# Stick-breaking attention of a decoder trunk on one core: prompt heads taken in pairs, and the sample heads' blocks taken one after the other while cache pages are read

## The chip, the core and the metric

The kernel runs on one core of one Trainium2 chip. The metric is the time of one execution on the device, in microseconds (us); lower is better. The kernel before was run three times: 3911.35, 3921.86 (the median) and 3925.43 us.

## What is computed

The reference runs a decoder trunk of four layers over two groups of requests that share weights: one prompt of 512 tokens, and eight samples of 8 tokens each (64 tokens in all). Width is 1024, with 16 heads of 64. Layers 0 and 3 mix tokens by a short convolution, layer 2 by a recurrence, and layer 1 by stick-breaking attention, which is what the change touches. Every layer ends in a convolution FFN of width 2816. The attention, cut to what matters:

```python
z = einsum('bqhd,bkhd->bhqk', q_blk, keys) * HEAD_DIM ** -0.5 + bias
mask = k_pos[None, :] < q_pos[:, None]
log_stay = where(mask, log_sigmoid(-z), 0.0)
between = cumsum(log_stay, axis=3, reverse=True) - log_stay
a = where(mask, exp(log_sigmoid(z) + between), 0.0)
o = einsum('bhqk,bkhd->bqhd', a, vals)
```

So the weight of a key depends on the sum of softplus(z) over all later keys. The prompt attends to itself; each sample attends to 256 cached keys, held in two pages of 128 keys that a page table names, and to its own 8.

## The kernel before

The program is written by hand for five engines (TensorE, VectorE, ScalarE, GpSimd and SyncE) that run their own instruction lists in order and meet at semaphores. On chip, keys lie on partitions and queries along the free dimension; everything in the attention is float32. A matmul instruction in float32 leaves two passes, that is two LDWEIGHTS and two MATMUL records, in the trace; a transpose leaves one.

**Prompt attention** (functions `attention` of each engine). A head has four pieces, one for each block of 128 keys, taken from the last block to the first. The piece of block kb has the queries from that block on, so the widths are 128, 256, 384 and 512 columns. There are 64 pieces, head after head. For a piece, TensorE computes the scores from 64 rows of K and Q (`scores`, L715); VectorE adds the head's bias (L1762) and takes the absolute value (L1764); ScalarE takes Exp and Ln (L1293, L1295); VectorE completes softplus into `SP` (L1773); GpSimd sets the masked half of the first 128 columns to zero (`mask_sp`, L2198). Then TensorE adds to the scores, in the same PSUM bank, the softplus sums within the block (`cumulate`, matrix `ntri`, L723) and those over all later blocks (matrix `nones`, L727). For the latter, GpSimd keeps a running sum over the blocks, `SUM`, with a copy and an add per piece (L2203, L2205). ScalarE takes Exp with the bias (`weights`, L1303), GpSimd masks the first 128 columns again (`mask_a`, L2215), and after four pieces TensorE multiplies by the values (`values`, L740), 64 columns of the array, and VectorE takes the result of two heads (L1779). TensorE's list runs scores two pieces ahead of the sums.

**Sample attention.** GpSimd loads the 16 key pages and then the 16 value pages (512 KB each) into four buffers `PG` (L2190). For each of the eight samples TensorE transposes both pages (L770), ScalarE copies each half page to `KTP` (L1205), and TensorE multiplies by the queries (L778): 16 matmuls of 16 columns. Only after the last page do the softplus, the masks and the sums of the three key blocks follow, over 1024 columns (16 heads by 64 tokens) each: the samples' own 64 keys (block 2), the second page (block 1) and the first page (block 0), with DVE L1800, L1813 and L1818, ACT L1323, L1325 and L1329, POOL L2227 and L2231, PE L788, L791 and L794. Then TensorE multiplies by the own values (L800) and by the 16 value pages (L809).

The order of the work is written out by hand in Python loops over the pieces, one for each engine; there is no planner.

## Time and profile before

| | |
|---|---|
| median of three runs | 3921.86 us |
| profiled execution, its own time | 3924.92 us |
| its span in the trace | 3923.2 us |
| mean granted TensorE clock, share of full speed | 0.932 |
| PE busy in matmuls | 3539.9 us (90%) |
| DVE / ACT / POOL busy | 1576.9 / 1298.6 / 410.5 us |
| instructions | 76827 |

The profile comes from one execution. PE is TensorE's matmuls and PEld its weight loads, DVE is VectorE, ACT is ScalarE, POOL is GpSimd. The granted clock is told as a share of 2.4 GHz: 1.00 is 2.4 and 0.50 is 1.2 GHz. A bracket in a row of the timeline holds the idle time before it and what ended it.

### The profile page before, as it was taken

Reading aid. Unit: us, or ns where it says so; the run is one execution under the profiler, and the core shown is the slowest. Engines: PE = TensorE matmul, PEld = TensorE weight load, DVE = VectorE, ACT = ScalarE, POOL = GpSimd, SP = SyncE. Lnnn points to the kernel's source line nnn. Section 1 sums busy time; section 2 is a strip of 40 time slices with the busy share of each in tenths; the row PEclk is TensorE's granted clock in tenths of the full one; section 3 lists DMA queues with packets and bytes.
Section 4 is the critical chain, followed back from the end, with each engine's and each line's share of the span. In section 5 each row is a group of like instructions: output and inputs, shape, how many; then the busy total and the mean of one; then the engine's idle time right before and its main releaser. Section 6 shows DMA issues by size and latency. Waiting matters only on the chain.

```text
span 3923.2 us, 76827 instructions
## 1 busy us (share of the span) xinstructions
PE 3539.9 (90%) x33232; PEld 3231.5 (82%) x33232; DVE 1576.9 (40%) x2263; ACT 1298.6 (33%) x2088; POOL 410.5 (10%) x862
## 2 busy tenths in 40 slices
PE   5998999989788789999688789988999989999996
PEld 3997999979336579999578678867999979889996
DVE  1435443231451244442534654454444244354422
ACT  2223443222442234442333322323444222244422
POOL 1000000000452100000000432300000000000000
PEclk9999999999797599999888799989999999989998
DMA  4554223353102242224432100014222444222221
GB/s 158 151 153 152 80 81 107 94 172 92 49 1 86 87 132 86 80 83 118 138 92 61 39 17 15 20 42 132 86 80 83 118 145 114 79 59 81 83 79 46
DMA packets 450251, 350.04 MB, mean 89 GB/s; under 512 B 14652, under 2 KB 417100, under 8 KB 449596
## 3 DMA queue, kind: packets, MB, share of 16 engines
q1 hardware_dynamic: 439776, 308.58, 26.6%
q0 software_dynamic: 9616, 35.34, 2.8%
q8 instruction: 208, 3.41, 0.4%
q10 hardware_dynamic: 608, 2.36, 0.2%
q14 instruction: 43, 0.35, 0.0%
HBM read 333.44 MB, written 12.79 MB: 88 GB/s over the span
## 4 chain that ended last, share of the span: by engine, by line
PE 83%; DVE 8%; issue 3%; POOL 2%; ACT 2%; DMA 2%; POOLq 0%; DVEq 0%; ACTq 0%
PE ps L593 58%; PE ps L891 6%; PE ps L817 3%; PE ps L818 2%; PE ps L819 2%; PE ps L659 2%; DMA raw<-in_ada_w 1%; PE ps L688 1%; PE ps L740 1%; PE ps L778 1%; DVE XMf L1838 1%; PE ps L604 1%; DVE XMl L1842 1%; PE ps L770 1%; PE ps L723 1%
## 5 line engine op out<-in xcount | busy, mean ns | idle before, releaser
L1590 DVE TENSOR_TENSOR SL<-raw,SH 128x1024 fp32r<-128x1024 f32 x408 | 500.5, 1227 | 1544.4 <-ACT SH L1205 1544.4
L1205 ACT ACTIVATE SH<-raw 128x1024 fp32r<-128x1024 f32 x408 | 432.2, 1060 | 1596.3 <-PE ps L593 1358.4
L593 PE MATMUL ps<-Uh,SH 128*128 128x288 f32 x3744 | 806.1, 297 | 1.5 <-DVE GP L2069 1.1
L593 PE MATMUL ps<-Uh,SL 128*128 128x288 f32 x3744 | 801.7, 296 | 0.0
L593 PE MATMUL ps<-Ul,SH 128*128 128x288 f32 x3744 | 801.0, 296 | 0.0
L593 PEld LDWEIGHTS ps<-Uh,SH 128*128 128x128 f32 x3744 | 602.4, 189 | 18.4 <-issue 16.9
L593 PEld LDWEIGHTS ps<-Uh,SL 128*128 128x128 f32 x3744 | 603.3, 189 | 0.0
L593 PEld LDWEIGHTS ps<-Ul,SH 128*128 128x128 f32 x3744 | 603.3, 189 | 0.0
L593 PE MATMUL ps<-Hh,SH 128*128 128x288 f32 x1792 | 390.7, 300 | 2.4 <-DVE Hl L1829 2.4
L593 PE MATMUL ps<-Hh,SL 128*128 128x288 f32 x1792 | 383.9, 296 | 0.0
L593 PE MATMUL ps<-Hl,SH 128*128 128x288 f32 x1792 | 383.7, 296 | 0.0
L593 PEld LDWEIGHTS ps<-Hh,SH 128*128 128x128 f32 x1792 | 287.7, 189 | 13.1 <-issue 12.5
L593 PEld LDWEIGHTS ps<-Hh,SL 128*128 128x128 f32 x1792 | 288.9, 189 | 0.0
L593 PEld LDWEIGHTS ps<-Hl,SH 128*128 128x128 f32 x1792 | 288.9, 189 | 0.0
L2162 POOL COPY TL<-GP 128x2 f32 (+1 forms) x104 | 45.5, 438 | 1425.4 <-ACT GP L1205 1065.6
L817 PE MATMUL ps<-XMh,SH 128*128 128x288 f32 x448 | 141.5, 316 | 36.8 <-DVE XMl L1842 36.8
L659 PE MATMUL ps<-raw,CT 128*32 128x256 f32 x1408 | 120.3, 428 | 42.6 <-DMA raw<-in_ada_w 42.4
L1742 DVE SCALAR_TENSOR_TENSOR CV<-GP,ST,CV 128x592 f32<-128x592 f32 x176 | 147.0, 835 | 25.6 <-DVE CV L1742 0.6
L818 PE MATMUL ps<-XMl,SH 128*128 128x288 f32 x448 | 137.1, 306 | 0.0
L819 PE MATMUL ps<-XMh,SL 128*128 128x288 f32 x448 | 136.3, 304 | 0.0
L1205 ACT ACTIVATE Hh<-Hf (+1 forms) x112 | 76.0, 685 | 170.4 <-DVE Hf L2102 108.2
L817 PEld LDWEIGHTS ps<-XMh,SH 128*128 128x128 f32 x448 | 89.0, 199 | 45.8 <-issue 36.3
(407 smaller groups left out, 4854.3 us busy)
## 6 DMA issues: line engine op xcount, KB each, us to landing
raw<-in_ada_w SPq DMA_DIRECT2D x176, 512.0 KB, 4.3
raw<-in_f_w_gu SPq DMA_DIRECT2D x176, 512.0 KB, 3.8
raw<-in_f_w_down SPq DMA_DIRECT2D x64, 448.0 KB, 3.8
raw<-in_a_w_in SPq DMA_DIRECT2D x48, 512.0 KB, 5.1
raw<-in_f_w_down SPq DMA_DIRECT2D x32, 512.0 KB, 4.1
raw<-in_b_w_qkv SPq DMA_DIRECT2D x24, 512.0 KB, 4.6
raw<-in_r_w_rkv SPq DMA_DIRECT2D x24, 512.0 KB, 4.2
PRE<-in_ada_w SPq DMA_DIRECT2D x4, 2048.0 KB, 25.4
```

The lines of the kernel that those rows point to most:

```text
L593: mm = pe.matmul(ps[:, b + h, 0:TH], w, a[:, k, h * TH:(h + 1) * TH], start=on, stop=off)
L604: mm = pe.matmul(ps[32 * g:32 * g + 32, SS, 0:TQ], ones[:], SQ[:, n % 2, g * TQ:(g + 1) * TQ], start=(k == 0), stop=(k == KT - 1), skip_gr ...
L659: mm = pe.matmul(ps[32 * g:32 * g + 32, ADA, 0:2 * P], CT[:, k, :], src[:, 2 * P * g:2 * P * g + 2 * P], start=(k == 0), stop=(k == KT - 1 ...
L688: mm = pe.transpose(ps[0:cols, bank, g * width:g * width + rows], a, ident[0:rows, 0:rows])
L817: pe.matmul(out, wh, hi[:, cols], start=start, stop=False)
L818: pe.matmul(out, wh, lo[:, cols], start=False, stop=False)
L819: return pe.matmul(out, wl, hi[:, cols], start=False, stop=stop)
L891: mm = lambda out, l, r, start=False: pe.matmul(out, l, r, start=start, stop=True, skip_group_check=True)
L1205: copy = lambda out, in_: act.activation(out, in_, ACT.Copy)
L1590: dve.tensor_tensor(SL[:, m.mod(2)], raw[:, n.mod(4)], SH[:, m.mod(2)].bitcast(F32), ALU.subtract)\
L1742: ins = dve.scalar_tensor_tensor(CV[:, 0:CW], src, w(tap), CV[:, 0:CW], ALU.mult, ALU.add)
L2162: pool.tensor_copy(tl[:, 0:HIST], GP[:, g, NP_TOK:NP_TOK + HIST])
```

## The change

**Prompt.** A piece now holds two heads, the even and the odd head of a pair, in two PSUM banks of a ring of three pairs of banks; there are 32 pieces. The two heads' score matmuls stand one after the other (rows 0 to 63 and 64 to 127 of the array), and so do their value matmuls for each block (columns 0 to 63 and 64 to 127). VectorE and ScalarE treat both heads in one instruction, of twice as many columns, save for Exp with the bias, which stays one per head. `SUM` and its GpSimd instructions go. In their place `SP` keeps all four blocks of a pair, and TensorE multiplies `nones` by each later block apart (`later_blocks`), ahead of the scores of a later piece. The bias is added by a TENSOR_TENSOR in place of a TENSOR_SCALAR. GpSimd's list has `mask_a` of a piece ahead of `mask_sp` of the next.

**Samples.** Pages are read in the order of blocks: the second page of all eight samples, then the first page of all. TensorE transposes page m and then scores page m-1. Softplus and sums of block 2 and of block 1 are placed between pages; those of block 0 come after the last key page, with four value pages ahead of them on TensorE.

The diff, cut to its core:

```diff
                 def scores(pc):
-                    h, kb = where(pc)
-                    r, w = 64 * (h % 2), NP_TOK - kb * P
-                    if due(pc - 3):
-                        pe.wait_ge(a_ready, pc - 3)
-                    pe.matmul(ps[:, pc % 4, 0:w], KF[r:r + HD, h // 2, kb * P:(kb + 1) * P],
-                              QF[r:r + HD, h // 2, kb * P:NP_TOK], start=True, stop=True).then_inc(z_ready, 1)
+                    p, kb, w, _ = block_cols(pc)
+                    if due(pc - 2):
+                        pe.wait_ge(a_ready, pc - 2)
+                    for h, hh in HEADS:
+                        mm = pe.matmul(ps[:, 2 * (pc % 3) + h, 0:w], KF[hh, p, kb * P:(kb + 1) * P], QF[hh, p, kb * P:NP_TOK],
+                                       start=True, stop=True)
+                    mm.then_inc(z_ready, 1)
...
+                    for h in range(2):
+                        mm = pe.matmul(ps[:, 2 * (pc % 3) + h, 0:w], ntri[:], spent(pc)[:, h], start=False, stop=True,
+                                       skip_group_check=True)
                     mm.then_inc(cum_done, 1)
...
+                def later_blocks(pc):
+                    p, kb, w, _ = block_cols(pc)
+                    if kb == 3:
+                        return
+                    pe.wait_ge(zb_ready, pc + 1)
+                    for h in range(2):
+                        for later in range(3 - kb, 0, -1):
+                            pe.matmul(ps[:, 2 * (pc % 3) + h, later * P:w], nones[:], spent(pc - later)[:, h], start=False,
+                                      stop=True, skip_group_check=True)
...
+                        _, _, w, at = block_cols(3 - kb)
+                        for h, hh in HEADS:
+                            mm = pe.matmul(ps[hh, 6 + p % 2, kb * P:NP_TOK], VT[:, kb, (2 * p + h) * HD:(2 * p + h + 1) * HD],
+                                           AT[:, p % 2, h, at:at + w], start=(kb == 0), stop=(kb == 3), skip_group_check=True)
...
-                        values(k // 4 - 2)
+                for k in range(2):
+                    scores(k)
+                for k in range(PIECES + 1):
+                    if k < PIECES:
+                        later_blocks(k)
+                        if k + 2 < PIECES:
+                            scores(k + 2)
+                        cumulate(k)
+                    if k % 4 == 0 and 4 <= k:
+                        values(k // 4 - 1)
...
+                def page_turned(m):
+                    pe.wait_ge(page_full[m % 4], 16 * (m // 4 + 1))
+                    for hh in range(2):
+                        if due(2 * m + hh - 1):
+                            pe.wait_ge(kt_free, 2 * m + hh - 1)
+                        for q in range(4):
+                            k = 4 * hh + q
+                            mm = pe.transpose(ps[:, 6 + hh, q * P:(q + 1) * P], PG[:, m % 4, k * P:(k + 1) * P], ident[:])
+                        mm.then_inc(kt_full, 1)
+                def page_scores(m):
+                    b, j = seq_of(m)
+                    pe.wait_ge(kt_free, 2 * m + 2)
+                    for k in range(KT):
+                        bank, cols = 2 * j + k // 4, slice(b * NT, b * NT + NT)
+                        out = ps[:, bank, k % 4 * P:k % 4 * P + P].rearrange("p (r c) -> p r c", r=2)
+                        mm = pe.matmul(out[:, :, cols], KTP[:, m % 2, k, :], QB[:, k, :, cols],
+                                       start=(bank not in opened), stop=True, skip_group_check=True)
+                        opened.add(bank)
                     mm.then_inc(kt_used, 1)
...
+                for m in range(NPG + 1):
+                    if m < NPG:
+                        page_turned(m)
+                    if m >= 1:
+                        page_scores(m - 1)
+                    if m == NPG // 2 - 1:
+                        sums_within(0)
+                    if m == NPG // 2 + 2:
+                        sums_of_later(1)
+                    if m == NPG - 2:
+                        sums_within(1)
...
+                pe.wait_ge(sa, 2)
+                for m in range(4):
+                    page_values(m)
+                sums_of_later(2)
+                sums_within(2)
+                for m in range(4, NPG):
+                    if m == NPG // 2:
+                        pe.wait_ge(sa, 3)
+                    page_values(m)
...
+                    if due(p - 1):
+                        act.wait_ge(av_done, p - 1)
+                    for h in range(2):
+                        ins = act.activation(AT[:, p % 2, h, at:at + w], ps[:, 2 * (pc % 3) + h, 0:w], ACT.Exp,
+                                             bias=BB[:, 2 * p + h:2 * p + h + 1])
+                    ins.then_inc(a_ready, 1)
...
+                for k in range(PIECES + 2):
+                    if k >= 2:
+                        weights(k - 2)
+                    if k < PIECES:
                         soft(k)
...
+                for m in range(NPG):
+                    for hh in range(2):
+                        act.wait_ge(kt_full, 2 * m + hh + 1)
+                        if due(m - 1):
+                            act.wait_ge(kt_used, m - 1)
+                        copy(KTP[:, m % 2, 4 * hh:4 * hh + 4, :], ps[:, 6 + hh, :].rearrange("p (g c) -> p g c", g=4))\
+                            .then_inc(kt_free, 1)
+                    if m == 1:
+                        sample_soft(0)
+                    if m == NPG // 2:
+                        sample_weights(0)
+                    if m == NPG // 2 + 2:
+                        sample_soft(1)
+                sample_weights(1)
+                sample_soft(2)
+                sample_weights(2)
...
-                    dve.tensor_scalar(z, ps[:, pc % 4, 0:w], BB[:, h:h + 1], None, ALU.add).then_inc(zb_ready, 1)
+                    dve.tensor_tensor(z, ps[:, 2 * (pc % 3):2 * (pc % 3) + 2, 0:w],
+                                      BB[:, 2 * p:2 * p + 2].rearrange("p (h o) -> p h o", o=1).broadcast_to([P, 2, w]), ALU.add)\
...
-                    if due(pc - 1):
-                        dve.wait_ge(cum_done, pc - 1)
-                    if due(pc - 1):
-                        dve.wait_ge(sum_ready, pc - 1)
-                    dve.scalar_tensor_tensor(SP[:, pc % 2, 0:w], ZB[:, pc % 2, 0:w], 0.0, EX[:, pc % 2, 0:w],
+                    if due(p - 1):
+                        dve.wait_ge(cum_done, 4 * (p - 1))
...
                     z, e = SZ[0:rows, q, :], SE[0:rows, q, :]
+                    if n == 0:
+                        dve.wait_ge(snew, 1)
+                    else:
+                        dve.wait_ge(kt_used, n * NPG // 2)
                     with_bias(z, bank, rows).then_inc(szb, 1)
...
-                    ins = pool.tensor_copy(SUM[:, pc % 2, 0:P], d)
-                    if kb < 3:
-                        ins = pool.tensor_tensor(SUM[:, pc % 2, P:w], SUM[:, (pc - 1) % 2, 0:w - P],
-                                                 SP[:, pc % 2, P:w], ALU.add)
-                    ins.then_inc(sum_ready, 1)
-                    pool.wait_ge(sum_ready, pc + 1)
+                    diagonal(spent(pc)[:, :, 0:P]).then_inc(spm_ready, 1)
...
+                for k in range(PIECES + 1):
+                    if k >= 1:
+                        mask_a(k - 1)
+                    if k < PIECES:
                         mask_sp(k)
...
-                for n in range(NB * NPAGE + 4, 2 * NB * NPAGE):
+                for n in range(2 * NPG):
+                    if n == 7:
+                        pool.wait_ge(ssp, 1)
+                        same_sequence(SZ[0:NS_TOK, 2, :]).then_inc(sspm, 1)
+                    if n == NPG // 2 + 5:
+                        pool.wait_ge(sa, 1)
+                        same_sequence(SE[0:NS_TOK, 2, :]).then_inc(sam, 1)
```

How the instructions stand now, in three places.

TensorE in the middle of the prompt attention, before, one head (L715 scores, L723 sums within the block, L727 sums over later blocks, L740 values):

```order
L740 MATMUL ps<-AT,VT 64x512
...
L715 MATMUL ps<-QF,KF 128x256
L723 MATMUL ps<-SP,ntri 128x512
L727 MATMUL ps<-SUM,nones 128x384
L715 MATMUL ps<-QF,KF 128x384
L723 MATMUL ps<-SP,ntri 128x128
```

and in the change (x2 is the two heads; L729 scores, L738 within, L750 over later blocks, L760 values):

```order
L750 MATMUL ps<-SP_97,nones 128x128
L750 MATMUL ps<-SP_97,nones 128x256
L750 MATMUL ps<-SP_97,nones 128x384
...
L729 MATMUL ps<-QF,KF 128x256 x2
L738 MATMUL ps<-SP_97,ntri 128x512 x2
L729 MATMUL ps<-QF,KF 128x384 x2
L738 MATMUL ps<-SP_96,ntri 128x128 x2
L760 MATMUL ps<-AT,VT 64x512 x2
```

The sums over later blocks moved ahead of the scores and grew from one matmul per head to as many as there are later blocks; the matmuls of the two heads stand side by side.

TensorE in the sample attention of the change (L793 transposes, L803 page scores, L831 and L818/L820 softplus sums, L861 own values, L842 value pages); before, all L778 rows stood ahead of the first sum, and all sums ahead of L800 and L809:

```order
L793 MATMUL ps<-ident,PG 128x128 x8
L803 MATMUL ps<-QB,KTP 128x2x8 x8
L831 MATMUL ps<-SZ,ntri 128x512 x2
...
L803 MATMUL ps<-QB,KTP 128x2x8 x16
L861 MATMUL ps<-SE,VT 64x64 x16
L842 MATMUL ps<-SE,PG 64x8 x64
L818 MATMUL ps<-SZ,nones 128x512
L820 MATMUL ps<-SZ,nones 128x512
...
L831 MATMUL ps<-SZ,ntri 128x512 x2
L842 MATMUL ps<-SE,PG 64x8 x192
```

Six of the twelve 512-column sums moved into the page loop, the other six behind the first four value pages.

## Rows read from the trace of the kernel before

**Rows 1.** The page, chain that ended last: shares of the span by engine.
```profile
PE 83%; DVE 8%; issue 3%; POOL 2%; ACT 2%; DMA 2%; POOLq 0%; DVEq 0%; ACTq 0%
```
**Rows 2.** Busy time in five stretches: us, PE, PEld, DVE, ACT, POOL, PEclk, DMA share, GB/s.
```profile
998.90:1213.10 214.20, 178.06 (x474) 80.65 (x474) 104.22 (x200) 87.31 (x192) 102.82 (x241) 0.86 0.00 1
1213.10:1218.20 5.10, 3.10 (x16) 2.79 (x16) 1.75 (x3) 0.00 (x0) 2.18 (x4) 0.75 0.72 247
1218.20:1296.70 78.50, 72.53 (x385) 66.53 (x384) 0.04 (x1) 18.93 (x32) 8.48 (x16) 0.61 0.37 118
1296.70:1333.20 36.50, 21.98 (x24) 5.70 (x24) 15.04 (x16) 8.46 (x8) 9.83 (x4) 0.52 0.00 0
1333.20:1363.80 30.60, 27.18 (x545) 26.60 (x544) 1.30 (x3) 1.06 (x1) 6.39 (x12) 0.59 0.61 209
```
**Rows 3.** Chain of waits over one head of the prompt: start us, us, what.
```profile
1079.23 0.63 PE ps L715 x2
1079.85 1.06 PE ps L723 x2
1080.91 0.66 PE ps L727 x2
...
1087.16 1.21 POOL SUM L2205
...
1088.79 2.37 PE ps L740 x8
1091.16 0.63 PE ps L715 x2
```
**Rows 4.** Groups by form, 1000 to 1212 us: busy us, mean ns, idle before.
```profile
L1303 ACT ACTIVATE AT<-ps,BB 128x512 f32<-128x512 f32 x16 | 10.8, 672 | 5.3 <-PE ps L727 5.3
L1303 ACT ACTIVATE AT<-ps,BB 128x256 f32<-128x256 f32 x16 | 7.3, 457 | 0.0
L2198 POOL TENSOR_SCALAR_AFFINE_SELECT SP<-SP 128x128 f32<-128x128 f32 x64 | 18.9, 295 | 98.1 <-DVE SP L1773 86.2 <-issue 11.8
```
**Rows 5.** Timeline of PE where matmuls on parts of the array stand together.
```profile
93.26 0.61 PE L659 MATMUL ps<-raw,CT 128*32 128x256 f32 x8
...
2266.64 0.71 PE L891 MATMUL ps<-AR,B__109 64*64 64x128 f32 x8 [13.46 <-DVE SF L1984]
2267.12 0.65 PE L891 MATMUL ps<-AR,K__108 64*64 64x128 f32 x8
```
**Rows 6.** Timeline near 1201 us: DVE and POOL at once.
```profile
1201.18 0.87 DVE L1764 SCALAR_TENSOR_TENSOR EX<-ZB 128x512 f32<-128x512 f32 x1
...
1201.57 0.63 POOL L2215 TENSOR_SCALAR_AFFINE_SELECT AT<-AT 128x128 f32<-128x128 f32 x1
```
**Rows 7.** Timeline of PE in the loop over key pages, two samples.
```profile
1229.53 4.14 PE L778 MATMUL ps<-QB,KTP 128*128 128x16 f32 x32 [0.69 <-ACT KTP L1205]
...
1238.01 7.01 PE L778 MATMUL ps<-QB,KTP 128*128 128x16 f32 x32 [0.69 <-ACT KTP L1205]
...
1244.85 3.81 PE L770 MATMUL ps<-ident,PG 128*128 128x128 f32 x16
...
1249.35 7.01 PE L778 MATMUL ps<-QB,KTP 128*128 128x16 f32 x32 [0.69 <-ACT KTP L1205]
```
**Rows 8.** Timeline behind the last key page: bias, Exp, mask, one sum.
```profile
1299.11 1.27 DVE L1800 TENSOR_TENSOR SZ<-ps,BB 128x512 f32<-128x512 f32 x2
...
1318.83 2.07 PE L788 MATMUL ps<-SZ,ntri 128*128 128x512 f32 x2
1319.46 2.02 POOL L2231 TENSOR_SCALAR_AFFINE_SELECT SE<-SE 64x1024 f32<-64x1024 f32 x1
...
1324.26 1.06 ACT L1329 ACTIVATE SE<-SE 128x1024 f32<-128x1024 f32 x1 [6.96 <-DVE SE L1800]
```
**Rows 9.** Timeline of PE at the own values and at nine value pages.
```profile
1333.21 1.15 PE L800 MATMUL ps<-SE,VT 64*64 64x64 f32 x32
...
1344.07 15.76 PE L809 MATMUL ps<-SE,PG 128*64 128x8 f32 x288 [1.13 <-DMA PG<-in_cache_v]
```

More of the change, by code:

```diff
@@ L781, in attention, with halves @@
                     mm.then_inc(kt_used, 1)
-                for q in (2, 1, 0):
+                def halves(n):
+                    q = (2, 1, 0)[n]
                     rows = NS_TOK if q == 2 else P
-                    for hh in range(2):
-                        out = ps[0:rows, (4, 2, 0)[2 - q] + hh, :]
-                        cols = slice(512 * hh, 512 * hh + 512)
-                        pe.wait_ge(sspm, 3 - q)
+                    return q, [(ps[0:rows, (4, 2, 0)[n] + hh, :], slice(512 * hh, 512 * hh + 512)) for hh in range(2)]
@@ new lines, in sums_of_later, with sums_within @@
+                def sums_of_later(n):
+                    q, parts = halves(n)
+                    pe.wait_ge(szb, n + 1)
+                    for out, cols in parts:
+                        pe.matmul(out, nones[0:NS_TOK, :], SZ[0:NS_TOK, 2, cols], start=False, stop=True, skip_group_check=True)
+                        if q == 0:
+                            pe.matmul(out, nones[:], SZ[:, 1, cols], start=False, stop=True, skip_group_check=True)
+                def sums_within(n):
+                    q, parts = halves(n)
+                    rows = NS_TOK if q == 2 else P
+                    if n == 0:
+                        pe.wait_ge(sspm, 1)
+                    else:
+                        pe.wait_ge(ssp, n + 1)
+                    for out, cols in parts:
@@ L795, in attention, with page_values @@
-                    mm.then_inc(scum, 1)
-                pe.wait_ge(kt_free, g)
+                    mm.then_inc(scum, 1)
+                def page_values(m):
+                    b, j = seq_of(m)
+                    n = NPG + m
+                    pe.wait_ge(page_full[n % 4], 16 * (n // 4 + 1))
+                    for h in range(NH):
+                        r, c = 64 * (h % 2), h // 2 * NS_TOK + b * NT
+                        mm = pe.matmul(ps[r:r + HD, 6, c:c + NT], PG[:, n % 4, h * HD:(h + 1) * HD],
+                                       SE[:, j, sc(h) + b * NT:sc(h) + (b + 1) * NT], start=False, stop=True,
+                                       skip_group_check=True)
+                    mm.then_inc(pages_used, 1)
```

214 lines of the change are left out of this document (61 added, 153 removed).

## The prediction

> **What bounds the kernel now.** I began with the shares of the chain that ended last: TensorE holds 83% of it [rows 1]. But a busy share says nothing about one stage, so I cut the attention into five stretches [rows 2]. The prompt attention lasts 214.2 us with TensorE busy 178.1, the loop over key pages 78.5 us with 72.5, the softplus part behind it 36.5 us with 22.0, and the value pages 30.6 us. The last two, 67.1 us, are the part where TensorE waits most. Nothing outside the attention moves in the instruction lists, so the change can only be worth what these stretches give.
>
> The chain over one prompt head shows what a head costs [rows 3]: from 1079.23 to 1091.16 us, 11.93 us, at the full granted clock. TensorE's own work on it is 0.63 + 1.06 + 0.66 + 2.37 us in four runs of matmuls; between them the chain runs through GpSimd, where one add to the running sum takes 1.21 us. So the prompt is bound by turns: TensorE for some 80% of a head, the masks and the running sum on GpSimd for the rest.
>
> **Prices.** From the same rows: 256 columns take 0.63 us, 512 take 1.06, and 384 behind a run of the same form 0.66. That is 0.21 us for a run plus 0.21 for each 128 columns (a float32 matmul with its two passes). At 1.2 GHz a 512-column matmul takes 2.07 us [rows 8], so there I price a run at 0.37 plus 0.43 per 128. ScalarE's Exp with bias is 0.67 us at 512 columns and 0.46 at 256 [rows 4]. A mask of 128 columns is 0.295 us [rows 4], one of 1024 takes 2.02 [rows 8]; on the line between them the new 256-column mask is 0.54.
>
> **Do two heads overlap on the array?** The trace of before has no such pair of 64-row matmuls, so it must be bounded: from no overlap to full overlap. Eight passes of 256 columns on four column strips took 0.61 us [rows 5]; one after the other they would take 8 x 0.21 = 1.7. So column parts overlap. The 64x64 rows are nearest to the scores: eight passes of 128 columns start 0.48 us before the next eight (2266.64 to 2267.12), where a pass costs 0.21 at 1.2 GHz and eight in series 1.7 us. Column halves alone would give 0.85; only rows and columns together give 0.48. I take full overlap for scores and values.
>
> **Prompt, step by step.** TensorE's list per piece is: sums over later blocks, scores two pieces ahead, sums within the block; the values of the last pair follow the first piece. I count from the end of one "within" to the next, at full clock. Path one is TensorE's own work. Path two is Exp with bias for both heads, then both masks (the mask of the weights stands ahead of the next softplus mask in GpSimd's list), then "within", and 0.4 for handoffs of some 0.1, an estimate from the gaps in the chain.
> - Piece of 128 columns: path two, 2 x 0.67 + 2 x 0.54 + 0.64 + 0.4 = 3.5.
> - 256: path one, values 2.37 (both heads in the time of one), later 0.64, scores 1.06, within 1.06, waits 0.3: 5.4.
> - 384: path two, 2 x 0.46 + 1.08 + 1.49 + 0.4 = 3.9.
> - 512: path one, later 12 x 0.21 + 0.21 = 2.77, scores 0.64, within 1.92, waits 0.3: 5.6.
>
> A pair thus takes 18.4 us, of which TensorE works 15.4, against 2 x 11.93 = 23.9. The added `nones` matmuls (20 units of 128 columns a pair, against 12) are in it. VectorE has per pair 3 x 2560 elements; a bias over 1024 takes 1.27 us [rows 8], so some 10 us, and ScalarE about the same: both lie beside TensorE. VectorE's new TENSOR_TENSOR for the bias costs nothing for the same reason; without that cover the 32 biases of 640 columns on average, at 0.8 us, would stand on the path with 25 us. Over eight pairs: 147 against 191 us, so 44 saved. The other 23 us of the stretch (start, last head, stretches at 1.2 GHz) stay, and since a pair has less waiting in which to hide a low clock, I add 3. **Prompt: 41 us saved.**
>
> **Samples.** In the loop, TensorE waits 0.69 us for the last copy of each sample's pages [rows 7], eight times: 5.5 saved, because it now scores page m-1 while page m is copied. Added are six 512-column sums. A sum costs 2.0 us at 1.2 GHz and 1.06 at full; the loop's mean granted clock is 0.61 [rows 2], so 10 us. The loop gets 4.5 longer. ScalarE's 2.1 us of Exp and Ln between two copies lie beside 3.5 us of page scores (half of 7.01). GpSimd's masks of some 5 us, ahead of the loads of pages 7 and 13, lie beside the four pages already loaded, at 5.4 us a page; behind them a page would be late by no more than that.
> Behind the last key page stand now: own values 1.5, four value pages at 15.76 / 9 = 1.75 [rows 9], six sums at 2.0, twelve value pages at 1.75: 41.5 us at 1.2 GHz, against 67.1. The chain for block 0 (bias 1.27, absolute value 1.2, Exp and Ln 1.06 each, softplus 1.2: 5.8) ends before four pages and four sums (15 us) are through. I take 40, as a part ran at full clock before. 27 saved. **Samples: 22.5 us saved.** From both sides: 31 if the sums fall into full clock, 12 if the pages come later than TensorE wants them.
>
> **Sum.** 41 + 22.5 = 63.5, from the profiled execution's 3924.9 us: 3861. The median of the runs is 3 us lower, so I predict 3858.
>
> **Rivals.**
> (a) The two heads do not overlap. Then the values cost 2.1 more and the scores 0.85 and 0.43 more in the TensorE-bound pieces: 3.4 a pair, 27 in all: 3885. Against it stand [rows 5]. 7%.
> (b) GpSimd's masks wait for VectorE. A mask beside a two-tensor VectorE instruction took 0.63 instead of 0.295 us, and that instruction 0.87 [rows 6]. VectorE's instructions are now twice as long, and both masks are on path two. If each of the two masks waits a further 1.0 us in the two pieces that path two bounds, that is 4 us a pair, 32 in all: 3890. For it: there is only one GpSimd queue. Against: the copy and the add for the running sum are gone. 10%. On this the Trainium skill, "SBUF — State Buffer", section "Who interferes with whom", says that a VectorE instruction with two SBUF inputs and a GpSimd instruction that reads SBUF exclude each other for the whole instruction; By that rule a mask can wait for one whole instruction of 1.2 us, four times a pair: 38 us in all, 3896. The trace agrees with it in kind: mask and VectorE instruction both stretch where they meet [rows 6].
> (c) Slower: the granted clock stays at 1.2 GHz through the attention, since a pair now fills the array otherwise. With runs at 0.37 plus 0.43 per 128 columns the steps become 4.1, 9.8, 7.0 and 10.9, a pair 32 us; the prompt then takes some 266 us, 52 more than before, and the samples gain 6: 3968. It decides from the share of low clock: the prompt's gain is gone when two thirds of its time is at 1.2 GHz, all gain above five sixths. Now the mean clock there is 0.86, so a bit over a quarter. In the page loop TensorE was busy 92% of the time at 0.61, so busyness alone does not hold the clock up. 4%.
> (d) The clock is higher than now in both parts: 15 us in the prompt and 8 in the samples more: 3835. 4%.
> The forecast itself: 75%.
>
> **How the numbers follow.** A measurement of this kernel can tell about 0.5%, 20 us, from no change. Forecast, (a), (b) and (d) all lie over 0.5% faster: with what is left for surprises, 0.91 faster, 0.04 same, 0.05 slower. The range takes in (d) and (b) and the bounds of the samples: 3834 to 3892.
>
> **What would show it.** Prompt attention of 170 to 177 us between VectorE's first bias and the first page load; a pair about 18.4 us at full clock; the two heads' score and value matmuls starting within a few ns; TensorE waiting on GpSimd in the pieces of 128 and 384 columns. Page loop near 83 us without the waits for copies, and about 40 us from the last key page to VectorE's copy of the result. Wrong if a score pair of 512 columns takes 2 us at full clock, if masks last over 1 us, or if the granted clock in the prompt falls under 0.7.

## The result, and the profile after

| | before | after |
|---|---|---|
| median of the runs, us | 3919.89 (4 runs) | 3834.35 (4 runs, 3829.13 to 3836.29) |
| profiled execution, its own time | 3924.92 | 3832.99 |
| its span | 3923.2 | 3831.3 |
| mean granted clock | 0.932 | 0.939 |
| PE busy | 3539.9 | 3480.1 |
| prompt attention | 214.2 | 149.5 |
| load of the queries | 5.1 | 5.4 |
| loop over key pages | 78.5 | 83.3 |
| from there to the copy of the result | 67.1 | 40.0 |

The ratio of the times is 0.9769, with a 95% interval of 0.9749 to 0.9789: 2.3% faster. The forecast had 3858 and a range from 3834. The direction was right and the gain some 24 us larger than forecast. By its median the result lies on the range's lower edge; by the ratio, times the 3921.86 us of before that the forecast started from, it is 3831, 3 us under it.

The same windows as in [rows 2], after (us, then busy time of PE, PEld, DVE, ACT, POOL, then PEclk, DMA share, GB/s; the last two rows of [rows 2] are one here):

```profile
998.52:1148.02 149.50, 121.02 (x564) 68.87 (x564) 85.40 (x105) 75.67 (x128) 33.12 (x65) 0.96 0.00 1
1148.02:1153.38 5.36, 3.51 (x16) 3.28 (x17) 1.75 (x3) 0.00 (x0) 2.04 (x4) 0.68 0.73 274
1153.38:1236.71 83.33, 82.99 (x399) 75.08 (x400) 10.97 (x12) 24.43 (x38) 16.53 (x20) 0.56 0.35 109
1236.71:1276.67 39.96, 38.68 (x556) 30.68 (x556) 5.03 (x6) 3.17 (x3) 6.37 (x12) 0.54 0.47 159
```

64.7 us of the gain are in the prompt, 27.1 behind the last key page, and 4.8 are given back in the page loop and 0.3 in the load of the queries: 86.7 of the 91.9 us by which the spans differ. The rest lies almost all behind the attention, in code that the change doesn't touch.

TensorE in the prompt, timeline of the change over one pair (start us, us, engine, line, operation; brackets hold the idle time before and its releaser). L729 is the scores, L738 the sums within the block, L750 those over later blocks, L760 the values; x4 is two heads by two float32 passes:

```profile
1024.71 1.13 PE L729 MATMUL ps<-QF,KF 64*128 64x512 f32 x4
1025.77 1.13 PE L738 MATMUL ps<-SP,ntri 128*128 128x256 f32 x4
1026.73 1.47 PE L750 MATMUL ps<-SP,nones 128*128 128x128 f32 x8
1028.14 0.49 PE L729 MATMUL ps<-QF,KF 64*128 64x128 f32 x4
1030.04 1.56 PE L738 MATMUL ps<-SP,ntri 128*128 128x384 f32 x4 [1.41 <-POOL SP L2263]
1031.44 2.76 PE L750 MATMUL ps<-SP,nones 128*128 128x128 f32 x12
1034.13 0.70 PE L729 MATMUL ps<-QF,KF 64*128 64x256 f32 x4
1034.76 1.98 PE L738 MATMUL ps<-SP,ntri 128*128 128x512 f32 x4
1038.10 0.92 PE L729 MATMUL ps<-QF,KF 64*128 64x384 f32 x4 [1.36 <-ACT AT L1362]
1038.95 0.71 PE L738 MATMUL ps<-SP,ntri 128*128 128x128 f32 x4
1039.59 2.38 PE L760 MATMUL ps<-AT,VT 128*64 128x512 f32 x16
1041.89 0.71 PE L750 MATMUL ps<-SP,nones 128*128 128x128 f32 x4
1042.54 1.13 PE L729 MATMUL ps<-QF,KF 64*128 64x512 f32 x4
```

Read two things in it. A score matmul of 512 columns for two heads takes 1.13 us and all values of two heads 2.38, against 1.06 for one matmul of 512 columns and 2.37 for the values of one head [rows 3]: the second head costs next to nothing. And from 1024.71 to 1042.54 a pair takes 17.83 us, with the same two waits in each: 1.41 us for GpSimd's mask ahead of the sums of the 384-column piece, and 1.36 us for ScalarE's weights ahead of the next scores in the step of the 128-column piece.

The first of these waits goes back to VectorE. The mask ahead had long ended; by its bracket, this one waited 0.88 us for VectorE's last softplus instruction (L1843):

```profile
1028.36 1.16 DVE L1843 SCALAR_TENSOR_TENSOR SP<-ZB,EX 128x768 f32<-128x768 f32 x1
1029.58 0.41 POOL L2263 TENSOR_SCALAR_AFFINE_SELECT SP<-SP 128x256 f32<-128x256 f32 x1 [0.88 <-DVE SP L1843]
```

GpSimd's masks by form (busy us, mean ns of one, idle before), the counterpart of the mask in [rows 4]; in front the mask of the weights, then that of softplus:

```profile
L2263 POOL TENSOR_SCALAR_AFFINE_SELECT AT<-AT 128x256 f32<-128x256 f32 x32 | 20.5, 641 | 98.0 <-ACT AT L1362 98.0
L2263 POOL TENSOR_SCALAR_AFFINE_SELECT SP<-SP 128x256 f32<-128x256 f32 x32 | 13.3, 415 | 22.2 <-issue 11.8 <-DVE SP L1843 10.4
```

And the granted clock in the prompt attention, where most surprise lies. These windows cut it by the granted clock, before:

```profile
998.90:1027.00 28.10, 22.54 (x38) 10.38 (x39) 13.16 (x26) 11.22 (x25) 10.65 (x26) 0.50 0.00 1
1027.00:1171.00 144.00, 122.14 (x345) 55.65 (x343) 72.64 (x141) 60.60 (x135) 72.60 (x168) 0.91 0.00 1
1171.00:1213.00 42.00, 33.38 (x94) 14.61 (x92) 18.34 (x33) 15.48 (x33) 19.56 (x47) 0.92 0.00 1
```

and after:

```profile
998.50:1010.00 11.50, 6.03 (x18) 3.94 (x19) 6.78 (x10) 4.29 (x8) 1.38 (x3) 0.51 0.00 0
1010.00:1148.00 138.00, 115.00 (x549) 64.93 (x547) 78.61 (x95) 71.37 (x120) 31.72 (x62) 1.00 0.00 1
```

Before, TensorE starts with 28 us at 1.2 GHz and falls back to it several times later; after, it is at 2.4 GHz from 1010 us to the end.

What that cost shows head by head. From the 384-column scores of one head to those of the next, the timeline of before gives 15.07, 13.55, 11.93, 12.76, 11.92, 11.94, 11.93, 11.93, 11.92, 14.10, 13.62, 13.63, 13.62 and 13.62 us. The waits for GpSimd are the same in a head of 13.6 us as in one of 11.93 (0.60, 0.91 and 0.73 us); it is the matmuls that are slower. In the chain of waits of before, the values of two late heads take 4.06 us, against 2.37 in [rows 3]:

```profile
1150.61 4.06 PE ps L740 x8
1164.23 4.06 PE ps L740 x8
```

These 14 steps make 181.5 us, 14.5 more than 14 heads of 11.93. After, all six steps from pair to pair are 17.83 or 17.84 us.

### The profile page after: what moved, and what is told of

Its sections match the earlier page's. It is cut to its first block, busy times and chain, and to the rows that moved or that the text cites. A ratio compares the mean times of both kernels' runs of the same rounds, so it can differ in the third digit from the quotient of the medians.

```text
span 3831.3 us, 76444 instructions
## 1 busy us (share of the span) xinstructions
PE 3480.1 (91%) x33328; PEld 3223.4 (84%) x33328; DVE 1557.9 (41%) x2167; ACT 1286.4 (34%) x2024; POOL 339.0 (9%) x686
## 4 chain that ended last, share of the span: by engine, by line
PE 84%; DVE 8%; issue 3%; DMA 2%; ACT 2%; POOL 1%; POOLq 0%; DVEq 0%; ACTq 0%
PE ps L610 59%; PE ps L950 6%; PE ps L876 3%; PE ps L878 2%; PE ps L877 2%; PE ps L676 2%; DMA raw<-in_ada_w 1%; PE ps L705 1%; DVE XMf L1905 1%; PE ps L738 1%; PE ps L621 1%; PE ps L803 1%; DVE XMl L1909 1%; PE ps L633 1%; PE ps L750 1%
```

## The experiments

Each kernel was run beside the kernel before on the same chip. "Prompt", "loop" and "tail" are the stretches of the table above, in the profiled execution.

| run | made from | ratio to before (95%) | median us | prompt (clock) | loop (clock) | tail |
|---|---|---|---|---|---|---|
| the change | | 0.9769 (0.9749 to 0.9789) | 3834.4 | 149.5 (0.96) | 83.3 (0.56) | 40.0 |
| prompt_only | before | 0.9848 (0.9829 to 0.9867) | 3858.1 | 149.4 (0.96) | 76.3 (0.63) | 66.3 |
| sample_only | before | 0.9932 (0.9913 to 0.9952) | 3895.7 | 223.4 (0.85) | 78.5 (0.60) | 37.4 |
| heads_no_sum | before | 0.9984 (0.9971 to 0.9997) | 3916.6 | 211.2 (0.89) | 76.6 | 69.2 |
| filler | before | 0.9972 (0.9962 to 0.9982) | 3908.7 | 200.8 (0.97) | 77.1 | 68.8 |
| values_apart | change | 0.9826 (0.9802 to 0.9851) | 3849.8 | 161.9 (0.96) | 83.6 (0.56) | 39.9 |
| scores_apart | change | 0.9865 (0.9844 to 0.9887) | 3866.4 | 181.9 (0.93) | 83.9 (0.56) | 40.1 |
| no_later | change | 0.9797 (0.9777 to 0.9817) | 3838.0 | 159.9 (0.75) | 76.9 (0.61) | 40.3 |
| mask_order | change | 0.9784 (0.9763 to 0.9806) | 3834.2 | 147.9 (0.96) | 85.2 (0.56) | 41.1 |
| pairs_with_sum | change | 0.9804 (0.9778 to 0.983) | 3845.8 | 164.1 (0.90) | 83.5 (0.56) | 39.8 |
| sums_first | change | 0.9767 (0.9744 to 0.9789) | 3827.4 | 149.2 (0.97) | 78.5 (0.60) | 39.8 |
| loop_filler | change | 0.9766 (0.9734 to 0.9798) | 3826.3 | 149.5 (0.96) | 63.5 (0.97) | 39.4 |
| no_later_filled | change | 0.9809 (0.9785 to 0.9832) | 3847.0 | 163.1 (0.85) | 76.9 (0.61) | 40.0 |
| no_later_512 | change | 0.9794 (0.9778 to 0.981) | 3841.2 | 153.9 (0.94) | 83.5 (0.56) | 38.6 |
| best_256 | change | **0.9707 (0.9693 to 0.972)** | 3806.6 | 147.9 (0.96) | 55.4 (1.00) | 36.9 |
| best_tail | change | 0.9743 (0.973 to 0.9756) | 3823.3 | 147.9 (0.96) | 79.2 (0.77) | 47.7 |

The steps from head to head, or from pair to pair, by the same scores (the first and last heads are left out):

| run | fastest step, us | slower ones, us |
|---|---|---|
| before | 11.93 (6 of 14) | 12.8 to 15.1 |
| sample_only | 11.93 (1 of 14) | 13.6 to 14.0 |
| heads_no_sum | 11.74 (7 of 14) | 13.2 to 13.4 |
| filler | 12.15 (all 14) | |
| the change, prompt_only | 17.83 (all 6) | |
| mask_order | 17.62 (all 6) | |
| values_apart | 19.38 (all 6) | |
| scores_apart | 21.26 (3 of 6) | 22.9 |
| pairs_with_sum | 18.21 (2 of 6) | 19.7 to 19.9 |
| no_later | 17.37 (1 of 6) | 18.5 to 19.5 |
| no_later_filled | 17.69 (3 of 6) | 20.3 to 21.7 |
| no_later_512 | 18.04 (all 6) | |

### The two halves alone

prompt_only takes the prompt part of the diff alone, sample_only the sample part.

> The change with the sample attention of before put back. Theory one (the two parts are independent and the trace of the change has them right: prompt 64.9 us shorter, samples 22 us): about 3920 - 65 to 69 = 3851 to 3855 us, with a granted clock near 1.00 in the prompt attention again. Rival (the high clock in the prompt of the change's one profile was luck): a mean clock of some 0.86 there and the forecast's 41 us, 3879 us.

> The kernel before with only the sample attention of the change. Theory one: 22 us saved, 3898 us, and the prompt attention stays at 214 us with a mean clock near 0.86. Rival (what follows or precedes the prompt decides its clock): the prompt gets shorter too, under 3885 us.

The halves add up: 0.0152 and 0.0068 are 0.0220 of the 0.0231 measured. The stages show each half's own price more sharply: the prompt 149.4 in the one, the tail 37.4 in the other. sample_only's prompt code is that of before, and yet took 9 us more, at a clock of 0.85: all but one of its heads took 13.6 us or more. So the time of the old prompt differs from execution to execution, and a few us of difference between two single profiles of it say nothing; every kernel with the change's pair loop as it stands had 149.2 to 149.5 us, at 0.96 or 0.97. The total of prompt_only is some us above what the trace's stages led me to expect.

### Is it the running sum, or the clock?

heads_no_sum keeps single heads but drops the running sum from GpSimd, as the change does:

```diff
-                    if kb < 3:
-                        pe.wait_ge(sum_ready, pc)
-                        mm = pe.matmul(ps[:, pc % 4, P:w], nones[:], SUM[:, (pc - 1) % 2, 0:w - P],
...
+                    for later in range(3 - kb, 0, -1):
+                        mm = pe.matmul(ps[:, pc % 4, later * P:w], nones[:], spent(pc - later),
```

filler leaves the kernel before as it is and adds one useless 128-column matmul to each of the 64 pieces, where TensorE waits for the mask:

```diff
+                    pe.matmul(ps[:, 7, 0:P], nones[:], QF[:, 0, 0:P], start=True, stop=True)
                     pe.wait_ge(spm_ready, pc + 1)
```

> The kernel before, single heads, but the running sum on GpSimd is gone and TensorE multiplies each later block by nones instead (10 units of 128 columns a head in place of 6). Theory W (the low clock in the prompt came with TensorE's waits for GpSimd): the waits shrink, the head takes about 11.2 us, the mean clock in the prompt rises over 0.95, stretch about 190 us, total near 3896. Theory P (it takes the pairs on the array to hold the clock, or the waits are not GpSimd's): mean clock stays near 0.86, stretch over 205 us, total over 3908.

> The kernel before with one useless matmul of 128 columns into a free bank ahead of each wait for the softplus mask (64 matmuls, 0.43 us each at full clock by the price of a run, 27 us of TensorE work, mostly inside its waits of some 2.2 us a head). Theory W (the clock follows how full TensorE's time is): mean clock in the prompt over 0.95 and the stretch of 214 us does not grow, perhaps 200. Theory P (pairs on the array hold it): clock stays at 0.86 and the stretch grows by 5 to 20 us.

For single heads the sum's removal takes 0.19 us off a head at full clock (11.74 against 11.93), 3 us for 16: the extra matmuls cost nearly what the wait did. The prompt was 3 us shorter too, but two executions of the old prompt differ by more than that; the total says 1 to 11 us. The clock was 0.89, and half of the heads still took 13.2 us or more, so the theory that shorter waits for GpSimd bring the clock up missed. The filler makes each head 0.2 us longer than one at full clock, 12.15, but then none takes more: the prompt is 13 us shorter (11 in the total, by the ratio, 7 to 15), for work that nobody needs. So it does not take pairs on the array to hold the clock. Windows of the prompt, heads_no_sum:

```profile
999.89:1211.11 211.22, 184.76 (x570) 93.37 (x570) 99.30 (x201) 88.89 (x192) 35.10 (x129) 0.89 0.00 1
```

and filler:

```profile
999.61:1200.38 200.77, 175.04 (x600) 89.38 (x600) 101.59 (x200) 88.85 (x192) 103.15 (x241) 0.97 0.00 1
```

With 126 more matmul records than before, TensorE is busy 3 us less, because they ran at a mean clock of 0.97 instead of 0.86. So the low clock cost the old prompt, in the profiled execution, at least these 13 us.

### Do the two heads overlap?

values_apart runs one head's values through all blocks, then the other's; scores_apart puts one useless two-column matmul over the whole array between the two heads' scores:

```diff
-                    for kb in range(4):
-                        _, _, w, at = block_cols(3 - kb)
-                        for h, hh in HEADS:
+                    for h, hh in HEADS:
+                        for kb in range(4):
+                            _, _, w, at = block_cols(3 - kb)
```

```diff
                     for h, hh in HEADS:
+                        if h == 0:
+                            pe.matmul(ps[:, 2 * (pc % 3) + 1, 0:2], nones[:], QF[:, 0, 0:2], start=True, stop=True)
```

> The change, but the value matmuls stand head after head instead of side by side. If the two heads overlap on the array by standing side by side (a run of 2.38 us for both), the run becomes 4.5 to 4.8 us at full clock, 2.2 us more in each of 8 pairs, 18 us in all: ratio to the kernel before about 0.981 (3848). If the overlap is worth nothing on the path: 0.977. Clock in the prompt by theory W: stays near 1.00, since TensorE is fuller.

> The change, but a matmul of 2 columns over the whole array stands between the two heads' scores, so that they can't run together. If they overlap now, a score run of 512 columns grows from 1.1 to some 2.1 us, and the two TensorE-bound pieces of a pair get 0.9 and 0.5 us longer plus the small matmul's own 0.3 each, about 2 us a pair, 16 in all, less what lies in waits: ratio 0.979 to 0.981. If they did not overlap before: 0.977 to 0.978.

A pair then takes 19.38 and 21.26 us, at full clock, instead of 17.83. The values, head after head, take 3.93 us instead of 2.38: apart, but not the 4.5 to 4.8 expected, and where the rest went stays open. In scores_apart the timeline shows each head at the price that both had together:

```profile
1063.53 0.70 PE L729 MATMUL ps<-QF,KF 64*128 64x256 f32 x2
1064.16 0.38 PE L732 MATMUL ps<-QF,nones 128*128 128x2 f32 x2
1064.47 0.70 PE L729 MATMUL ps<-QF,KF 64*128 64x256 f32 x2
```

The prompt is 12.4 and 32.4 us longer; the second is twice what I had expected. Of it, 32 separating matmuls of 0.31 us (1064.16 to 1064.47) are some 10 us, and about 5 more went with the clock, which was 0.93 there: eight pairs of 21.26 would be 27.4 us over the change. This is rival (a) made to happen: about 12 and 17 us, 30 in both, where it had 27.

### Does TensorE's work hold its own clock up?

no_later takes the sums over later blocks away (`later_blocks` returns at once), with nothing in their place. no_later_filled puts a useless matmul of 256 columns ahead of every piece's scores instead, no_later_512 two of 512 ahead of every other piece's:

```diff
+                    if pc % 2 == 0:
+                        for h in range(2):
+                            pe.matmul(ps[:, 2 * (pc % 3) + h, :], nones[:], QF[:, 0, 0:NP_TOK], start=True, stop=True)
```

> The change without the nones matmuls in the prompt attention: the sums over later blocks are left out. By my steps the 256 and 512 pieces are bound by TensorE and lose 0.64 and 2.77 us, to what path two then allows (512 columns: 2 x 0.58 + 2 x 0.41 + 1.9 + 0.4 = 4.3 instead of 5.6); a pair goes from 17.8 to about 16 us at full clock, 14 us saved in all: ratio 0.973. Theory W: TensorE has more waits then (about 12 of 16 us busy, 75%), so the clock falls in part of the pairs, as in the kernel before, and the gain is lost: mean clock near 0.88 and ratio 0.977 or more.

> The change without the nones matmuls in the prompt (sums over later blocks left out) and with one useless matmul of 256 columns ahead of each piece's scores instead. Theory W: the clock goes back to 0.95 or more and the prompt from 159.9 to about 145 us, ratio near 0.975. If the clock had nothing to do with the missing work: clock stays near 0.75 and the prompt grows by up to 32 x 0.6 to 1.2 us, over 170.

> Leaves out the softplus sums over later blocks, as before, and puts two useless 512-column matmuls ahead of the scores of every piece of 128 or 384 columns: 32 of them, some 34 us at full clock, about what the sums cost, against 7 us of filler in the run with 256 columns. If the granted clock follows how much TensorE streams, the prompt attention comes back to a clock of 0.95 or more and to 148 to 155 us, with TensorE busy some 120 to 145 us. If the clock had fallen because of where the gaps lie and not for want of work, it stays at 0.85 or under and the prompt takes 165 us or more.

The windows of the prompt in the three, in this order:

```profile
999.82:1159.77 159.95, 110.94 (x372) 47.26 (x372) 85.37 (x104) 75.58 (x128) 32.44 (x65) 0.75 0.00 0
```

```profile
1001.26:1164.36 163.10, 118.07 (x430) 52.06 (x430) 85.39 (x104) 75.73 (x128) 33.32 (x65) 0.85 0.00 1
```

```profile
997.65:1151.50 153.85, 114.88 (x428) 48.86 (x428) 84.77 (x105) 75.67 (x128) 33.10 (x65) 0.94 0.00 1
```

Taking 192 of 564 matmul records away went with a prompt 10 us longer, in the one profile of each: the clock fell from 0.96 to 0.75. The totals of no_later and the change (3838.0 and 3834.4, with intervals that overlap) do not tell them apart; the loop of no_later's profile was 6 us shorter. The 14 us that I expected to save were not there either: its fastest pair took 17.37 us, not 16. What the useless matmuls took is in the groups by form, first no_later_filled:

```profile
L728 PE MATMUL ps<-QF,nones 128*128 128x256 f32 x58 | 22.9, 480 | 24.7 <-ACT AT L1361 24.7
```

then no_later_512:

```profile
L730 PE MATMUL ps<-QF,nones 128*128 128x512 f32 x56 | 27.8, 618 | 16.0 <-ACT AT L1363 16.0
```

(The 7 us that the last expectation gives the smaller filler is the difference of PE's busy time; the group shows 22.9.) With the first the clock came back only to 0.85, a miss of that expectation, and it paid for its own time; with the second to 0.94, just short of the 0.95 expected, and the prompt to 153.9, with TensorE busy 114.9 us where I had 120 at least. TensorE still waited 16.0 us for ScalarE ahead of these fillers, so these waits alone did not bring the clock down. More useless work went with a higher clock, 0.75, 0.85 and 0.94 in order; but the fillers also differ in place and in shape, and which of these counts is not told apart.

### GpSimd's part

mask_order puts the softplus mask of a piece ahead of the weight mask of the piece before; pairs_with_sum brings the running sum back into the pair loop, for both heads at once, with one `nones` matmul a head.

```diff
                 for k in range(PIECES + 1):
-                    if k >= 1:
-                        mask_a(k - 1)
                     if k < PIECES:
                         mask_sp(k)
+                    if k >= 1:
+                        mask_a(k - 1)
```

```diff
+                    ins = pool.tensor_copy(SUM[:, pc % 2, :, 0:P], spent(pc)[:, :, 0:P])
+                    if kb < 3:
+                        ins = pool.tensor_tensor(SUM[:, pc % 2, :, P:w], SUM[:, (pc - 1) % 2, :, 0:w - P],
+                                                 spent(pc)[:, :, P:w], ALU.add)
```

> The change with GpSimd's softplus mask of a piece ahead of the weight mask of the piece before. Rival (b) says that two masks in a row stand on the path in the pieces of 128 and 384 columns: one mask of 0.41 us less in each, with what it waits for VectorE 0.8, so 0.8 to 1.6 us a pair, 6 to 13 us in all: ratio 0.974 to 0.975. If the masks are not what bounds: 0.977.

> The change with the running sum back on GpSimd (copy and add for both heads, one nones matmul per head and piece, softplus kept for two pieces only). It tells what the pairs are worth without the change of the sums. If the pairs bring the gain: TensorE works 1.7 us less a pair, GpSimd some 6 us more; the prompt stays at 150 to 155 us if GpSimd's turns lie beside TensorE, 0.977 to 0.979. If the sums' leaving GpSimd was needed: adds of up to 768 columns (1.0 to 1.2 us for 256 to 384 before, so 2 to 3 us here) stand before the masks, and a pair takes 20 to 23 us, 20 to 40 us lost: 0.982 to 0.987.

mask_order saves 1.6 us of the prompt (0.21 us in each pair), nothing that the total can tell, and not the 6 to 13 of rival (b). Its weight masks no longer meet VectorE's instructions (groups by form):

```profile
L2263 POOL TENSOR_SCALAR_AFFINE_SELECT SP<-SP 128x256 f32<-128x256 f32 x32 | 13.2, 413 | 112.3 <-DVE SP L1843 100.5 <-issue 11.8
L2263 POOL TENSOR_SCALAR_AFFINE_SELECT AT<-AT 128x256 f32<-128x256 f32 x32 | 13.0, 406 | 13.8 <-ACT AT L1362 13.8
```

406 ns instead of 641: the stretched masks are real, but all of them were worth 1.6 us. pairs_with_sum makes the prompt 14.6 us longer, at 0.90, between the two cases of its expectation. At full clock the running sum costs little in pairs as well: the fastest pair took 18.21 us, 0.4 more than in the change, 3 us for eight. Most of the 14.6 us lies in the pairs of 19.7 to 19.9 us, at the lower clock: what the new way of summing brings is mainly that the clock stays up.

### The samples

sums_first has the six sums of block 0 ahead of the first value pages. loop_filler adds one useless matmul of 512 columns a key page. best_256 has one of 256 columns there, and mask_order's edit; best_tail the 512 columns, mask_order's edit, and one more useless matmul ahead of every second value page.

```diff
-                for m in range(4):
-                    page_values(m)
                 sums_of_later(2)
```

```diff
+                        if hh == 0:
+                            pe.matmul(ps[:, 6, 0:256], nones[:], QF[:, 0, 0:256], start=True, stop=True)
                         for q in range(4):
```

```diff
+                    if m % 2 == 0:
+                        pe.matmul(ps[:, 7, :], nones[:], QF[:, 0, 0:NP_TOK], start=True, stop=True)
```

> The change with the six sums of block 0 directly behind the own values, ahead of the first four value pages. By my step the chain for block 0 (5.8 us on VectorE and ScalarE) is hidden behind the four pages; ahead of them TensorE waits first 1 us for the bias and then, behind four sums of 8 us, not at all, so only the loads of later pages start later (the first pages_used comes 12 us later): 0 to 4 us lost, 0.977 to 0.978. Rival: the pages' order matters, since the value pages then come four at a time from memory behind the sums: 8 us lost, 0.979.

> The change with one useless matmul of 512 columns into the transposes' bank ahead of each key page's transposes. The page loop runs at 1.2 GHz (mean clock 0.56) although TensorE is busy 99.6% of it, with matmuls of 16 columns and weight loads. Theory W2 (columns streamed hold the clock, not busy time): clock over 0.85, a page 3.3 + 0.85 us, six sums 6.4, the loop 73 to 76 us instead of 83: ratio 0.974 to 0.975. Theory B (the clock in the loop is low for another reason): the loop gets 16 x 1.7 = 27 us longer, 0.984.

> The change, with the softplus mask ahead of the weight mask on GpSimd, and one useless 256-column matmul ahead of each key page's transposes, half the filler of the run that held the clock. If 256 columns a page are enough, the page loop has a clock of 0.9 or more and lasts 58 to 64 us against 83.3, and the median is 3810 to 3822; if they are not, the loop stays near 0.6 and is 2 us longer than in the change, 3836.

> The change, the softplus mask first, one useless 512-column matmul for each key page, and one more ahead of every second value page. If the clock rises in the value pages too, the two sums there take 1.06 instead of 2.07 us each and the pages 0.9 instead of 1.75, and the stretch behind the last key page ends at what the loads of 12 value pages leave: 30 to 36 us against 40.0, median 3805 to 3815. If the loads already bound that stretch, it stays at 38 to 41, and the median is that of the loop filler, 3815 to 3826.

sums_first lost nothing: the tail took 39.8. The four value pages that the change puts ahead of those sums hide nothing that this run can show. Its loop, with the code of the change, took 78.5 us against 83.3: the full clock lasted for more of the first pages. Over all kernels with this loop it was 76.9 to 85.2 us.

In the change, the first pages take 2.6 us at full clock, and from 1160 us on, though TensorE did not wait, one page takes 5.01 us at 1.2 GHz; two pages of its timeline (L793 transposes, L803 scores):

```profile
1212.69 1.95 PE L793 MATMUL ps<-ident,PG 128*128 128x128 f32 x8
1214.43 3.43 PE L803 MATMUL ps<-QB,KTP 128*128 128x16 f32 x16
1217.70 1.95 PE L793 MATMUL ps<-ident,PG 128*128 128x128 f32 x8
1219.44 3.43 PE L803 MATMUL ps<-QB,KTP 128*128 128x16 f32 x16
```

In best_256 a page takes 3.09 us with the useless matmul (L792) in it:

```profile
1158.34 0.68 PE L792 MATMUL ps<-QF,nones 128*128 128x256 f32 x2
1158.85 1.04 PE L795 MATMUL ps<-ident,PG 128*128 128x128 f32 x8
1159.72 1.86 PE L805 MATMUL ps<-QB,KTP 128*128 128x16 f32 x16
1161.43 0.68 PE L792 MATMUL ps<-QF,nones 128*128 128x256 f32 x2
```

The loop and the tail in windows, best_256:

```profile
1150.78:1206.18 55.40, 55.06 (x429) 49.65 (x429) 10.03 (x12) 23.22 (x38) 17.30 (x20) 1.00 0.52 171
1206.18:1243.07 36.89, 34.93 (x557) 27.54 (x556) 5.03 (x6) 3.17 (x3) 6.34 (x12) 0.62 0.52 173
```

It beats both kernels: 0.9707, with an interval wholly below that of the change. Its median of 3806.6 is below the 3810 that I had as the lower end, and the loop below its 58 us.

The larger fillers are less clear. loop_filler's one profile had a loop of 63.5 us at 0.97, shorter than I had expected of it, yet its times run from 3816 to 3835 and its ratio is that of the change. best_tail's profile shows how: in pieces of the same loop the full clock was there, was lost, and did not come back for long:

```profile
1165.00:1180.00 15.00, 15.00 (x107) 12.20 (x106) 0.00 (x0) 4.34 (x8) 2.38 (x5) 1.00 0.49 152
1180.00:1200.00 20.00, 20.00 (x107) 14.79 (x106) 5.45 (x6) 7.38 (x11) 6.92 (x6) 0.81 0.30 100
1200.00:1216.00 16.00, 16.00 (x58) 12.72 (x59) 0.00 (x0) 2.39 (x4) 1.06 (x2) 0.50 0.30 95
```

TensorE was busy in every us of them. So a filler there does not guarantee the clock, and why the 256 columns did better than the 512 in these executions stays open. In best_tail the tail took 47.7 us where I had expected 30 to 36, and the median of 3823.3 lay above the 3805 to 3815; but the profiled execution was this kernel's slowest, 3834.5 us, so that 0.77 and 47.7 may be worse than usual. The first four value pages (two of them here), fillers and all, ran at 1.2 GHz; where the clock did rise, TensorE waited for the loads:

```profile
1233.63 2.07 PE L843 MATMUL ps<-QF,nones 128*128 128x512 f32 x2
1235.63 3.59 PE L846 MATMUL ps<-SE,PG 128*64 128x8 f32 x64
...
1264.92 1.13 PE L843 MATMUL ps<-QF,nones 128*128 128x512 f32 x2 [0.66 <-DMA PG<-in_cache_v]
1268.30 2.08 PE L843 MATMUL ps<-QF,nones 128*128 128x512 f32 x2
```

## Where the prediction was wrong, and what of it held

**Overlap of two heads.** Right, in full. The Trainium skill, "TensorE: Matmul & The Clock Gate", Part 3 on packing small matmuls, says that matmuls on different tiles of the array run at once; this trace agrees for both row and column halves, at two float32 passes each, 1.13 us for two heads' 512 columns and 2.38 for their values.

**A pair.** 18.4 us forecast, 17.83 measured. TensorE waits in the pieces of 128 and 384 columns only, as forecast, but not for what was forecast. By the ends of the "within" matmuls the four pieces take 2.9, 5.1, 4.7 and 5.1 us, for 3.5, 5.4, 3.9 and 5.6, so that misses of up to 0.8 us cancel in part. Path two, both Exp and then both masks, bounds neither: at 128 columns TensorE waits for the Exp of the 512-column piece before it can start the next scores, and at 384 for a mask that waits for VectorE, which I had put beside TensorE at no cost. The prices of 0.21 us a run and 0.21 for each 128 columns held (the 12 `nones` passes of the 512-column piece took 2.76 us; by the prices 12 x 0.21 + 0.21 is 2.73, not the 2.77 written). One reading was loose: the four runs of 0.63 to 2.37 us are a part of TensorE's work on a head, and the 80% is right (9.75 of 12.0 us busy). Eight pairs give 142.6 us for the forecast's 147: 4.6 of the missing 24.

**The rest of the prompt stretch.** This is the step that failed: "The other 23 us of the stretch (start, last head, stretches at 1.2 GHz) stay, and since a pair has less waiting in which to hide a low clock, I add 3." They did not stay. After, 149.5 less 142.6 leaves 6.9 us, so 16.4 of the 23 went and the 3 never came: 19 us, most of the miss. Of the 16.4, 14.5 are the heads of before that took more than 11.93 us, and 2 lie at the start and the end. I had treated the low clock as a fixed loss of the place, while it went with the old code: after, no pair behind the first is slowed. The filler run gives the mechanism from one side (the old code at 0.97 is 13 us shorter, and no head takes over 12.2 us), no_later and pairs_with_sum from the other (the new code with less TensorE work in it has pairs over 1 us slower than its fastest). What in a kernel's TensorE work decides the clock stays open. In the forecast this was rival (d), "the clock is higher than now", at 4%; it came true in the prompt (15 us there forecast) and not in the samples. My argument on it, that busyness alone does not hold the clock up, was right, and I drew nothing from it for the prompt, where the change has 564 matmul records in 149.5 us (3.8 a us) and before had 474 in 214.2 (2.2), though a higher clock raises that rate by itself.

**The samples.** Loop 83 forecast, 83.3 measured; tail 40 and 40.0. The terms were right: the waits for copies are gone (TensorE idle for 0.3 us of 83.3), and the six sums take 10.9 us in the loop, for 10 forecast. That the sum is right to the us is luck, since the same loop took from 76.9 to 85.2 us in other profiles, by how long the full clock lasted at its start. The forecast took this clock as given; best_256 shows that it was not, at 28 us of this loop.

**Rival (b), masks waiting for VectorE.** Of its 32 us, the order of the masks gives back 1.6. (With the other order TensorE still waits there 1.2 us a pair, for VectorE to finish the softplus and not for a mask that meets it.) The Trainium skill, "SBUF — State Buffer", section "Who interferes with whom", would have had a mask wait for a whole VectorE instruction; the rows show a mean of 641 ns against 406 without the meeting, and no more than 965 ns for one, so the trace agrees with the contention but not with 1.2 us added to each. **Rival (a)** was excluded by the overlap, **rival (c)** by the granted clock of 0.96 (its step of 256 columns comes to 10.4 us by its own prices, not 9.8, some 5 us in all).

**The range.** Its lower end stood on (d) alone, with 15 us for the prompt and 8 for the samples, and no room for the pair to be cheaper than costed. Those two together make the 24 us.

## What to carry to other kernels

When a stretch shows a granted clock between the two levels, cost it as its own term and ask whether the change alters what TensorE streams there; do not carry it over as fixed. Before costing a wait that you remove, try the cheapest test of the clock: a useless matmul in a bank that is free, inside the wait; where it shortens the stretch, the low clock was costing more than the filler. And test such a filler with several timed runs, since one profile at full clock does not say that every execution has it.

## What was not expected of the hardware

- TensorE busy 99.6% of a stretch (82.99 of 83.33 us, 16-column matmuls and transposes) had a granted clock of 0.56; with 256 columns of useless matmul a page it was 1.00 and the page 3.09 us instead of 5.01, filler and all.
- With less work a stretch was longer: 192 matmul records fewer, 10 us more, at 0.75 instead of 0.96, in one profile of each.
- The same code with the same waits ran at two speeds: heads of 11.93 and of 13.62 us in one execution of before, and almost only the slower ones in another kernel with the same prompt code.
- With TensorE busy throughout, best_tail's page loop still fell from full clock to 1.2 GHz, and best_256's, with half the useless columns a page, did not.
